# A transformer block on one core: a third home for the weights of the seven block products, and two weight sums made by an accumulating DMA

## The reference

```python
u = rmsnorm(h, norm_attn_pre); z = u @ w_in          # to qa, ka, va, qb, kb, vb, ga, gb
ya = diff_attention(...); yb = swa_sink_attention(...)
mix = sigmoid(ga) * (ya @ w_branch_a) + sigmoid(gb) * (yb @ w_branch_b)
h = h + rmsnorm(mix @ w_out, norm_attn_post)
u = rmsnorm(h, norm_ff_pre)
f = square(relu(u @ w_ff1)) @ w_ff2                  # 2048 -> 8192 -> 2048
h = h + rmsnorm(f, norm_ff_post)
```

## Time and profile before

| | us |
|---|---|
| median of 3 runs | 1325.58 |
| the profiled execution | 1325.52 |
| its span | 1323.7 |
| TensorE matmul busy | 1311.4 (99%) |
| VectorE busy | 928.1 (70%) |
| ScalarE busy | 671.0 (51%) |
| GpSimd busy | 47.0 (4%) |
| HBM read | 249.29 MB, 190 GB/s |

### The profile page before, as it was taken

One profiled execution on the slowest core, in us unless ns is written; L12 is line 12 of the kernel. 1 busy time (PEld: TensorE's weight loads), 2 busy tenths in 40 slices (PEclk: granted clock), 3 DMA queues, 4 the chain that ended last, 5 costly groups with the idle time before them and its releaser, 6 DMA issues.

```text
span 1323.7 us, 18258 instructions
## 1 busy us (share of the span) xinstructions
PE 1311.4 (99%) x6998; PEld 1116.4 (84%) x6998; DVE 928.1 (70%) x1265; ACT 671.0 (51%) x922; POOL 47.0 (4%) x92
## 2 busy tenths in 40 slices
PE   9999999999999999999999999999999999999998
PEld 8889999888888888889987888877888877888886
DVE  7766565687875555557768976579876699776554
ACT  7554453456664443454645664445454455545442
POOL 1222110000000000000000000000000000000000
PEclk9999999999999999999999999999999999999999
DMA  9766555555566666674755666646576465766653
GB/s 315 205 185 170 170 163 149 167 167 155 170 194 188 185 188 221 226 246 148 219 159 188 214 219 191 195 156 207 190 223 189 146 207 191 229 188 190 223 195 104
DMA packets 135209, 252.56 MB, mean 191 GB/s; under 512 B 8275, under 2 KB 45551, under 8 KB 134748
## 3 DMA queue, kind: packets, MB, share of 16 engines
q1 hardware_dynamic: 131216, 241.40, 58.6%
q0 software_dynamic: 2160, 4.74, 1.8%
q10 hardware_dynamic: 1756, 5.36, 1.1%
HBM read 249.29 MB, written 2.17 MB: 190 GB/s over the span
## 4 chain that ended last, share of the span: by engine, by line
PE 90%; DVE 6%; ACT 2%; DMA 1%; issue 0%; ACTq 0%; SPq 0%; DVEq 0%
PE bank L2006 16%; PE bank L1696 11%; PE bank L1698 11%; PE bank L1697 11%; PE bank L2009 8%; PE bank L1742 4%; PE bank L2056 4%; PE bank L2057 4%; PE bank L2058 4%; PE bank L1730 3%; PE bank L1731 3%; PE bank L1729 3%; PE bank L1744 2%; DVE b_lo L1536 2%; DVE s_lo L1541 1%; ACT b_hi L873 1%
## 5 line engine op out<-in xcount | busy, mean ns | idle before, releaser
L1017 DVE TENSOR_TENSOR w_lo<-raw,w_hi 128x1024 fp32r<-128x1024 f32 (+1 forms) x360 | 430.6, 1211 | 247.6 <-ACT w_hi L559 246.1
L559 ACT ACTIVATE w_hi<-raw 128x1024 fp32r<-128x1024 f32 (+1 forms) x360 | 372.4, 1048 | 292.9 <-DMA raw<-in_w_ff 173.5
L2006 PE MATMUL bank<-f_hl,w_hi 128*128 128x512 f32 x960 | 229.7, 391 | 0.0
L2006 PEld LDWEIGHTS bank<-f_hl,w_hi 128*128 128x128 f32 x960 | 176.4, 188 | 34.1
L2009 PEld LDWEIGHTS bank<-f_hl,w_lo 128*128 128x128 f32 x960 | 123.1, 191 | 4.7
L2009 PE MATMUL bank<-f_hl,w_lo 128*128 128x256 f32 x960 | 124.5, 283 | 0.0
L1696 PE MATMUL bank<-w_hi,u_hl 128*128 128x512 f32 x256 | 101.1, 395 | 0.0
L1698 PE MATMUL bank<-w_hi,u_hl 128*128 128x512 f32 x256 | 99.9, 390 | 0.0
L1697 PE MATMUL bank<-w_lo,u_hl 128*128 128x512 f32 x256 | 99.8, 390 | 0.0
L873 ACT ACTIVATE b_hi<-b_raw 128x2048 fp32r<-128x2048 f32 x24 | 46.1, 1921 | 72.7 <-DVE b_raw L1528 72.7
L1730 PE MATMUL bank<-u_hl,w_lo 128*128 128x272 f32 x288 | 82.4, 289 | 0.4 <-DVE w_lo L1017 0.4
(11 more groups left out here) (282 smaller groups left out, 2314.7 us busy)
## 6 DMA issues: line engine op xcount, KB each, us to landing
raw<-in_w_ff SPq DMA_DIRECT2D x160, 512.0 KB, 4.0
raw<-in_w_in SPq DMA_DIRECT2D x128, 512.0 KB, 3.7
s_raw<-in_w_ff SPq DMA_DIRECT2D x48, 512.0 KB, 3.9
b_raw<-in_w_ff SPq DMA_DIRECT2D x24, 1024.0 KB, 5.1
raw<-in_w_out SPq DMA_DIRECT2D x32, 512.0 KB, 4.3
raw<-in_w_branch_b SPq DMA_DIRECT2D x16, 512.0 KB, 3.8
raw<-in_w_branch_a SPq DMA_DIRECT2D x16, 512.0 KB, 3.8
xt<-in_turned_x SPq DMA_DIRECT2D x8, 272.0 KB, 5.4
```

The costliest lines, as they stand in the source:

```text
L559: act.activation(w_hi[:, u, :, 0:width], raw[:, u, :, 0:width], ACT.Copy).then_inc(hi_ready, 1)
L1017: dve.tensor_tensor(w_lo[:, u, :, 0:width], raw[:, u, :, 0:width], w_hi[:, u, :, 0:width].bitcast(F32), ALU.subtract).then_inc(lo_ready, 1)
L2006: ins = pe.matmul(acc[g][:], w_hi[:, u, k, cols], f_hl[:, kt, :], start=kt == 0, stop=kt == KT - 1)
```

## The change

A third home for quads, `b_raw2`, lies over `h2`; `h2` is stored in HBM before and loaded back in quarter 3. The homes of the eight quads are 2, 0, 1, 2, 0, 1, 0, 2. Quad 0 and single row 0 are loaded before the last chunk's units. There are still two `b_hi`, so ScalarE waits for the quad two before. `load_w` has a second DMA: row 4j+1's second half goes into slot 4 as well. GpSimd then adds slots 1 and 2 to slots 3 and 4 by an accumulating DMA within SBUF, in place of VectorE's `sum`. Signs of the sums, of the hidden tiles and of the joining are turned to fit.

```diff
+B_SLOT = [2, 0, 1, 2, 0, 1, 0, 2]
+B_BEFORE, B_NEXT, B_COUNT = ...   # per home: quads before, next quad, count
-HI_ORDER = [("first", 0), ("rest", 0), ("S", 0), ("S", 1), ("first", 1), ("rest", 1), ("S", 2)]
-LO_ORDER = [("sum", 0), ("sums", 0), ("first", 0), ("rest", 0), ("S", 0), ("S", 1), ("sum", 1), ("sums", 1), ("first", 1),
+HI_ORDER = [("first", 0), ("rest", 0), ("S", 0), ("first", 1), ("S", 1), ("rest", 1), ("S", 2)]
+LO_ORDER = [("sums", 0), ("first", 0), ("rest", 0), ("S", 0), ("S", 1), ("sums", 1), ("first", 1),
             ("rest", 1), ("S", 2)]
 for _k in range(2, N_W):
     HI_ORDER += [("first", _k), ("S", 2 * _k - 1), ("rest", _k), ("S", 2 * _k)]
-    LO_ORDER += [("sum", _k), ("S", 2 * _k - 1), ("sums", _k), ("first", _k), ("rest", _k), ("S", 2 * _k)]
+    LO_ORDER += [("S", 2 * _k - 1), ("sums", _k), ("first", _k), ("rest", _k), ("S", 2 * _k)]
...
+    h2_kept = nc.dram_tensor("h2_kept", (P, BLOCKS, D), F32)
...
+            [("b_raw2", [P, 7, CW], F32)], [("b_lo2", [P, 7, CW], F32R)])     # in the region of h2
...
# SyncE
             def load_w(q, k, free):
...
+                sp.dma_start(b_raw[i][:, 4, :], w_ff2[0, bass.ds(q * D + (4 * j + 1) * P, P), slice(c * 1024 + CW, c * 1024 + 1024)])\
+                  .then_inc(b_landed[i], 16)
...
             def load_ff2(q):
                 before = uses_before(q)
-                load_s(q, 0, None)
-                load_w(q, 0, before + 24 + 4)
-                load_w(q, 1, before + 24 + 7)
+                load_w(q, 1, before + 24 + 4)
+                load_w(q, 2, before + 24 + 7)
                 load_s(q, 1, before + 24 + 8)
                 for i, it in enumerate(ORDER):
...
-                    if it[0] == "W" and n + 2 < N_W:
-                        load_w(q, n + 2, before + 32 + i + 1)
+                    if it[0] == "W" and B_NEXT[n]:
+                        load_w(q, B_NEXT[n], before + 32 + i + 1)
...
             def quarter(q, first=False):
                 load_first(q, first)
                 for j in range(1, 4):
+                    if j == 3:
+                        if first:
+                            sp.wait_ge(norm, 6)
+                            sp.wait_ge(h2_stored, 16)
+                        load_s(q, 0, None)
+                        load_w(q, 0, None if first else uses_before(q))
...
             q = QUARTERS - 1
             load_first(q)
             for j in range(1, 4):
+                if j == 2:
+                    sp.dma_start(h2[:], h2_kept.ap()).then_inc(h2_landed, 16)
...
# GpSimd
+            for q in range(QUARTERS - 1):
+                for k in range(N_W):
+                    i = B_SLOT[k]
+                    pool.wait_ge(b_landed[i], b_lands(q, k, 32))
+                    pool.dma_start(b_raw[i][:, 3:5, :], b_raw[i][:, 1:3, :], accum_op=ALU.add).then_inc(b_added[i], 16)
...
# ScalarE, "first"
-                    act.wait_ge(b_landed[n % 2], 16 * (n // 2 + 1) + q * (16 * N_W // 2))
+                    act.wait_ge(b_landed[B_SLOT[n]], b_lands(q, n, 32))
+                    act.wait_ge(used, uses_before(q) + (24 + 4 + 3 * n if n < 2 else 32 + W_AT[n - 2] + 1))
...
# ScalarE, chunk_ff1
+                    if first and j == 1 and u == UNITS - 1:
+                        act.wait_ge(stats, 6 + 8)
+                        act.dma_start(h2_kept.ap(), h2[:]).then_inc(h2_stored, 16)
...
# ScalarE, split_next (the next quarter's first units)
+                    act.wait_ge(used, uses_before(q) + 32 + W_AT[N_W - (1 if u >= 3 else 2)] + 1)
...
# VectorE
-                if kind == "sum":
-                    dve.wait_ge(b_landed[i], 16 * (n // 2 + 1) + q * (16 * N_W // 2))
-                    dve.tensor_tensor(raw_b[:, 4:2:-1, :], raw_b[:, 3:0:-2, :], raw_b[:, 2:4, :], ALU.subtract)\
-                       .then_inc(b_part, 1)
-                elif kind == "sums":
...
+                if kind == "sums":
+                    dve.wait_ge(b_added[i], b_lands(q, n, 16))
+                    dve.tensor_tensor(raw_b[:, 5, :], raw_b[:, 1, :], raw_b[:, 4, :], ALU.add).then_inc(b_part, 1)
+                    dve.wait_ge(b_part, n + 1 + q * N_W)
+                    dve.tensor_tensor(raw_b[:, 6, :], raw_b[:, 0, :], raw_b[:, 5, :], ALU.add).then_inc(b_ready, 1)
...
# VectorE at the end, and TensorE's last product
+                dve.wait_ge(h2_landed, 16)
...
+                    pe.wait_ge(h2_landed, 16)
```

More of the change, by code:

```diff
@@ L88 @@
 S_COUNT = [S_SLOT.count(a) for a in range(3)]
+B_SLOT = [2, 0, 1, 2, 0, 1, 0, 2]
+B_BEFORE = [B_SLOT[:n].count(B_SLOT[n]) for n in range(N_W)]
+B_NEXT = [next((m for m in range(n + 1, N_W) if B_SLOT[m] == B_SLOT[n]), None) for n in range(N_W)]
+B_COUNT = [B_SLOT.count(a) for a in range(3)]
 LAST_W = [max(i for i in W_AT if ORDER[i][1] == c) for c in range(2)]
@@ L317, in hybrid_block @@
         o_squared, hg_part, hg_ready = sem("o_squared"), sem("hg_part"), sem("hg_ready")
-        b_landed = [sem(f"b_landed{i}") for i in range(2)]
+        b_landed = [sem(f"b_landed{i}") for i in range(3)]
+        h2_stored, h2_landed = sem("h2_stored"), sem("h2_landed")
+        b_added = [sem(f"b_added{i}") for i in range(3)]
         s_landed = [sem(f"s_landed{i}") for i in range(3)]
@@ L364, in uses_before, with b_lands @@
             return 8 * C_FF + q * USES
+        def b_lands(q, n, each):
+            return each * (B_BEFORE[n] + 1 + q * B_COUNT[B_SLOT[n]])
         def hi_no(q, kind, n):
@@ L432, in load_w @@
                 _, c, j = ORDER[W_AT[k]]
-                sp.wait_ge(used, free)
-                sp.dma_start(b_raw[k % 2][:, 0:4, :].rearrange("p (k h) n -> p k (h n)", k=2),
+                if free is not None:
+                    sp.wait_ge(used, free)
+                i = B_SLOT[k]
+                sp.dma_start(b_raw[i][:, 0:4, :].rearrange("p (k h) n -> p k (h n)", k=2),
                              unit_of(w_ff2, bass.ds(q * D + 4 * j * P, 2 * P), slice(c * 1024, c * 1024 + 1024)))\
-                  .then_inc(b_landed[k % 2], 16)
+                  .then_inc(b_landed[i], 16)
+                sp.dma_start(b_raw[i][:, 4, :], w_ff2[0, bass.ds(q * D + (4 * j + 1) * P, P), slice(c * 1024 + CW, c * 1024 + 1024)])\
+                  .then_inc(b_landed[i], 16)
             def load_s(q, n, free):
@@ L449, in load_first @@
                 before = uses_before(q) - len(ORDER)
-                last0, last1 = max(W_AT[0::2]), max(W_AT[1::2])
-                freed = {u: last0 for u in range(3)} | {3: max(last0, last1)} | {u: last1 for u in range(4, 7)} | {7: max(S_AT[n] for n in range(N_S) if S_SLOT[n] == 1)}
+                last = [W_AT[max(n for n in range(N_W) if B_SLOT[n] == i)] for i in range(2)]
+                freed = {u: last[0] for u in range(3)} | {3: max(last)} | {u: last[1] for u in range(4, 7)} | {7: max(S_AT[n] for n in range(N_S) if S_SLOT[n] == 1)}
                 for u in range(UNITS):
@@ L1481, in activate_hidden @@
                 dve.wait_ge(hid_part, n + 1)
-                dve.tensor_tensor(work[:, 8, :], work[:, 3, :], work[:, 1, :], ALU.add).then_inc(hid_part, 1)
+                dve.tensor_tensor(work[:, 8, :], work[:, 3, :], work[:, 1, :], ALU.subtract).then_inc(hid_part, 1)
                 dve.wait_ge(hid_part, n + 2)
@@ L1486, in activate_hidden @@
                 dve.wait_ge(hid_part, n + 3)
-                dve.tensor_tensor(work[:, 10, :], work[:, 0, :], work[:, 9, :], ALU.subtract).then_inc(hid_ready, 1)
+                dve.tensor_tensor(work[:, 10, :], work[:, 0, :], work[:, 9, :], ALU.add).then_inc(hid_ready, 1)
             def keep_hidden(q, j, last):
@@ L1515, in split_item @@
             def split_item(q, kind, n):
-                i = n % 2
-                lo, hi, raw_b = b_lo[i], b_hi[i], b_raw[i]
-                part = 2 * n + q * (2 * N_W)
-                if kind == "sum":
-                    dve.wait_ge(b_landed[i], 16 * (n // 2 + 1) + q * (16 * N_W // 2))
-                    dve.tensor_tensor(raw_b[:, 4:2:-1, :], raw_b[:, 3:0:-2, :], raw_b[:, 2:4, :], ALU.subtract)\
-                       .then_inc(b_part, 1)
-                elif kind == "sums":
[L1525 to L1528, removed]
+                i = B_SLOT[n % N_W]
+                lo, hi, raw_b = b_lo[i], b_hi[n % 2], b_raw[i]
+                if kind == "sums":
[3 more added lines that the diff above has]
+                    dve.tensor_tensor(raw_b[:, 6, :], raw_b[:, 0, :], raw_b[:, 5, :], ALU.add).then_inc(b_ready, 1)
                 elif kind == "first":
@@ L1565, in join @@
                                       for b in range(BLOCKS) for h in range(2)]
-                dst, other = ((c11, p1), (p6, p1), (p7, p6), (c21, p7), (p6, p5), (c12, p6), (p7, p5), (c22, p7))[step]
+                dst, one, other = ((c11, c11, p1), (p6, p6, p1), (p7, p7, p6), (c21, c21, p7), (p6, p5, p6), (c12, c12, p6),
+                                   (p7, p5, p7), (c22, c22, p7))[step]
                 if step:
                     dve.wait_ge(p_part, step)
```

(4 more changed lines are left out.)

12 lines of the change are left out of this document (7 added, 5 removed).

## The result

The changed kernel takes **1335.08 us** (median of 4 runs, 1334.91 to 1336.66) against 1325.68 (4 runs, 1325.39 to 1327.54) on the same chip: ratio 1.0069, 95% interval 1.0056 to 1.0083. Forecast were 1319.8 and the range 1316.0 to 1328.5; it is slower, by 9.4 us. The profiled execution took 1334.91.

A forecast was written before the change was run, and what follows sets the result against it. TensorE was taken as the bound, its matmuls filling 1311.4 of 1323.7 us, so only its standstill could be won. Sum: 1325.5 - 10.5 + 1.8 (quad 1) + 3.0 (quad 6) = 1319.8 us, range 1316.0 to 1328.5.

The forecast's parts named there:

- the stages' 10.5 us: TensorE's waits in the three block stages: 255.57 us against 245.1 without waits, the most the change could win.
- Left at quad 1: At each block stage's start, single row 1 still loads late, so quad 1's low part keeps TensorE waiting, 1.8 us in sum.
- The add's landing: GpSimd's 512 KB accumulating DMA within SBUF, issue to landing: 6.4 us, between bounds of 3.9 and 9.6.
- Quad 6's wait: In each block stage, quad 6's load and add in sequence make TensorE wait 1.0 us, 3.0 in all.
- The residual stream's way out and back: Store before chunk 3 hidden by 2.7 us, reload under quarter 3's first products: no cost.
- the one on DMA load: Block stages' DMA share rises from 0.61 to 0.85 to 1.0; 4 us of cover protect single rows, so no cost taken.
- one to two microseconds a stage: Cost in a block stage if single rows' loads lose their cover; held to lie within the range, not in the sum.
- without a new wait: 10.5 - 1.8 = 8.7 gained: Gain in the three block stages if only quad 1's 1.8 us of waits stay and no new one comes.
- The joining's waits: VectorE's joining of results in block stages: its later waits go, with 1.2 us less VectorE work in each period.
- The slower case: Block stages slower because quad 6's add bounds them, from 8.4 us landing; 1329.4 us at the high bound; chance 0.2, slower outcome 0.19.
- The second rival: At quad 6, an add of 7.5 to 9 us or lengthening DMA queues: three waits of 2.1 to 3.6, 1323 to 1327.5; chance 0.18.
- The signs list: Profile signs of a wrong forecast: add over 8 us, gaps at quads 1 to 5, VectorE waiting for rows, chunk 3 gap.

The follow-up runs named there:

- the pair of copies: Changed kernel with two plain 512 KB DMAs within SBUF in place of each accumulating DMA, VectorE waiting for both: 1337.87 us, ratio 1.0091 against the kernel before.
- one copy: Changed kernel with a plain 512 KB DMA within SBUF in place of each accumulating DMA: 1323.47 us, ratio 0.9979 against the kernel before.
- the reordering that made it longer: Third home with VectorE's sums, no adds; quad 1's sums before the last hidden chunk, row 3 before its low part and quad 2's sum: 1329.42 us, ratio 1.0021.

## Why the prediction was wrong

**Where it was right.** That the prize is the stages' 10.5 us, and that quad 0's share of it, 3.5, would go. Left at quad 1: forecast 1.8, measured 2.3. The add's landing: forecast 6.4, median 6.0. Quad 6's wait: forecast 3.0, measured 3.5, though some 2.0 of it stand at the quad's first product, for the first low part (950.59, L1561), and not at the fourth as forecast, so the nearness of the number is in part luck. The residual stream's way out and back: forecast nothing, measured nothing. With these alone, and the rest of the waits gone as forecast, the result would have been 1325.5 - 10.5 + 2.3 + 3.5 = 1320.8.

**The step that failed** is the one on DMA load: "Single rows have 10 us from free place to use, of which landing and splitting take 6.2, so 4 us cover them. I take nothing". It has three faults.

The first is a count that doesn't hold for all rows: rows 2 and 3 take the homes of rows 0 and 1 (`S_SLOT` begins 0, 1, 0, 1, 2), so 33 matmuls (7.5 us) lie between free place and use, and not 45 (10.2). The load of row 2 goes out at 890.32 and TensorE wants its first high part, without waits, at 882.49 + (2 x 21 + 2 x 12) x 0.227 = 897.5: 7.2 us, and 6.2 of it were spoken for. One microsecond of cover, not four, at the row that the hidden chunk follows.

The second is the landing time, taken as if the queue were free. Quad 3's load is ahead of row 2 and quad 2's add beside it, and ScalarE got the row 6.6 us after its issue instead of 3.7. Both take part: moving the load took the rows' wait from 5.0 to 1.4, leaving out the add to nothing.

The third is that "one to two microseconds a stage" closed the matter for a lost cover. Against the same kernel without the add, 13.4 us of waits came: 5.0 at rows 1 and 2, 4.8 at quads 1 to 4 and 3.5 at quad 6. Only the last was in the sum; the others are 3.3 a stage. Part of it is row 2's lateness carried on (hidden chunk, SyncE's stop, quad 4's and row 5's loads, VectorE's queue), which puts quad 3's last low part from 33.7 to 35.6 us after the stage's start. It isn't paid a second time at quad 3, since TensorE comes there as much later. The link from row 5 to quad 3 is shown by the sums put ahead of it; the one through SyncE's stop rests on the timelines and on its waits (22.3 with the add and 22.1 with the pair of copies, 16.4 with one copy, 15.6 with none), and isn't shown by itself, since no kernel took that stop alone away; the reordering that made it longer (7.9 us) put 11.3 us on quad 2.

**A second step that failed** stands in the gain. The words "without a new wait: 10.5 - 1.8 = 8.7 gained" need all later waits gone, quad 3's 1.1 too. The kernel without the add is that case, and it gained 5.6 us (1326.32 less 1320.74). Quad 3's wait of 4.6 was in no term: as a column half's last quad it needs its second low part at its second product, and VectorE's list has that only behind row 5, whose load ScalarE gets 7.3 us after its issue (896.21 to 903.55) where the kernel before took 5.1. With quad 6's wait on top, as forecast, this case comes to 1320.7 + 3.0 = 1323.7 and not 1319.8.

**The price that was sized by the wrong unit.** The prediction counted an add as 0.52 to 1.05 MB at 311 GB/s, 1.7 to 3.4 us of the engines. The measured 2.8 lies inside, and the forecast share of 0.85 to 1.0 is even a little over the 0.79 to 0.81 measured. So the load was known; what it does to landings with little cover was not worked out. The average share hides it; the 10 us windows show it.

**The joining's waits** (quad 4) were to go with VectorE's relief: they were 1.8 and are 2.4. The relief by itself does take them away: without the add they are 0, and quad 1's wait is 1.5 instead of 3.4. Quad 3 takes most of that back (4.6 instead of 0.5), so no sum and no add at all (1320.74) stands only 1.8 us below the home with VectorE's sums (1322.57). That is what the relief bought in this order of work, and the add costs 14.3.

**The rivals.** The slower case was given 0.19, and its mechanism, quad 6's add over 8.4 us, is not what happened: VectorE got quad 6's data 6.3 to 7.0 us after the issue. The second rival ("the add eats the gain"), for which the single rows' loads were named, was placed at quad 6 too. The signs list did name "gaps at quads 1 to 5, VectorE waiting for single rows"; they should have been a rival with a price.

The Trainium skill (DMA: Bandwidth & Descriptors, Anatomy of one DMA — SWDGE (gpsimd) path) fits such a transfer as 2.0 us plus bytes over 436 GB/s, which gives as an estimate 2.0 us for 16 KB and 3.2 for 512 KB. Only the quickest transfers here come near that: 2.0 for 16 KB and 2.8 for a plain copy of 512 KB. The medians lie above it, 3.1, 5.1 and 6.0 for the add, in stages whose engines are 0.65 to 0.8 busy. So the prediction was right not to take the page's 3.2 for the sum.

## What to carry to other kernels

Before work is moved from a compute engine to DMA, list each load in the stage with its own cover, from free place to first use, and with the bytes ahead of and beside it; here it was the loads with the least cover that set the price, not the average share. Then follow what a late one carries with it: which instruction stands behind it on its engine, and which queue waits for that. And test the parts of a change apart, since here one half gained some 3 us and the other lost over 12.

## What the runs showed of the hardware that was not expected

- An accumulating DMA of 512 KB within SBUF holds the 16 DMA engines 2.8 us, 2.2 times the 1.27 us of a plain copy of the same bytes (188 against 413 GB/s of bytes written); it lands in 6.0 against 5.1 us. GpSimd's instruction that issues it takes 0.85 us, the copy's 0.53.
- A long wait is paid again in clock. Behind the 7.26 us that TensorE stood in quarter 2 of the kernel with later quad loads, the next eight distances of matmuls are 0.43 us instead of 0.23, some 1.6 us lost. The granted clock is 0.50 from 1114.4 to 1117.4, the lower level of 1.2 GHz, and 0.80 in the 10 us window. TensorE's timeline and the window:

```profile
1114.35 0.63 PE L2091 MATMUL bank<-b_lo,hid_hi 128*128 128x512 f32 x1
1114.78 0.63 PE L2092 MATMUL bank<-b_hi,hid_lo 128*128 128x512 f32 x1
...
1105.00:1115.00 10.00, 2.74 (x10) 1.99 (x9) 7.40 (x8) 5.18 (x4) 0.85 (x1) 0.80 0.90 267
```
